# Two mixers with their order of work changed: recurrence first, attention second, in a one-core decoder trunk

## The chip, the cores and the metric

The kernel runs on one core of a Trainium2 chip. The metric is the device time of one execution in microseconds (us), median of several runs. A core has TensorE (PE in the profile: matrix products and transposes; PEld is its weight load), VectorE (DVE), ScalarE (ACT), GpSimd (POOL) and SyncE (SP, which here issues the weight transfers). Each engine works its own instructions off in the order in which they are written and waits on semaphores for the others.

## The reference

A trunk of two layers on 256 tokens of width 1024, all in fp32. The part that matters here is the mixer at the head of each layer:

```
u = rmsnorm(h, mix_norm_gain[i])
fq, fk, fv, fg, hq, hf, hi, hg = split(u @ w_in[i])
a_out = head_rmsnorm(forgetting_attention(fq, fk, fv, fg, bias), fox_gain, 8)
r_out = head_rmsnorm(hgrn2_recurrence(hq, hf, hi, lower_bounds[i]), hgrn_gain, 8) * silu(hg)
h = h + concatenate([a_out, r_out]) @ w_out[i]
```

The attention ("FoX" below) has 8 heads of 64 and a decay from the cumulated gate added to its logits. The recurrence ("HGRN") has 8 heads too: its output at t sums q_t k_s v_s over s <= t, each product decayed elementwise by the forget gates between s and t. After the mixer layer 0 has a dense SwiGLU of width 2816, layer 1 a top-2 mixture of 8 experts of width 3584; each layer ends with a gated embedding, and the trunk with a norm.

## The kernel before, in words

**Products.** Every fp32 matrix is split in a high and a low part in a reduced format, and a product is three matmuls (lines 1427 to 1429). Weights arrive as chunks of 1 MB in 7 buffers (`raw`), in the order of the list `STATIC`. Of each chunk ScalarE makes the high part (`hi_upto`, L562) and VectorE the low part (`lo_upto`, L878); SP may load chunk n only after chunk n-7 has been consumed. Tokens are 2 tiles of 128 (`t`).

**Projections of a mixer.** Of the seven 512-wide projections the gate `hg`, `fv` and `hi` are made token-major, in four quarters of 12 matmuls (a token tile and half the contraction each, `quarter`); `hf`, `fq`, `fk`, `hq` are made transposed, each in two chunks of 48 matmuls over all 256 tokens (`transposed`), between whose halves other work of TensorE can be put (`between`).

**Recurrence.** The chunkwise sum is done by levels: `step(0)` and `step(1)` make the diagonal of the score matrix of each token tile, `step(2)` to `step(8)` the blocks of 1, 2, 4 ... 64 tokens behind each other, `step(9)` the part across the two tiles. For each step TensorE does 16 or 32 small matmuls, VectorE masks the result into `scores` (`take`), and between two levels it multiplies the keys and queries by the decay over the span (`decay`, two instructions); a step waits for the decay of the level before. `recur(t)` then multiplies the scores by `hi`.

**Attention.** `pair_logits(i)` makes the logits of two of six units, VectorE finds the row maxima (`unit_max`), ScalarE the exponentials (`unit_exp`), TensorE turns them (`pair_turn`), ScalarE copies them out (`pT_out`), `attend(t)` multiplies by `fv`.

**Heads and output.** For each of four head tiles j (half, t) ScalarE squares, VectorE sums (`mean_square`), ScalarE makes the root (`head_root`), VectorE normalizes (`head_norm`, for the HGRN half with the gate besides), TensorE turns the tile (`head_turn`), VectorE multiplies by the gain (`head_gained`), ScalarE and VectorE split it (`head_hi`, `head_rest`). An `out_part(n, hf, t)` is 12 matmuls: output half n, contraction half hf, token tile t. After the last head tile the sum h of token tile 0 is formed (`add_to_h`) and normalized for the next stage (`norm(1, 0)` in layer 0, `norm_gained(0)` in layer 1, both write `un`); TensorE turns `un`, then does one more `out_part`.

**Order.** Everything is written out by hand, one list per engine: `mixer(l)` of ScalarE at L608, of VectorE at L1002, of TensorE at L1455. TensorE's list was: `hf`, `fq`, `fk`, `hq` with the logits of attention in between; then the quarters of `fv` and `hi` with the steps of the recurrence, `attend(0)` and `attend(1)` between them; head tiles in the order FoX 0, FoX 1, HGRN 0, HGRN 1; `out_part` of contraction half 0 (FoX) first.

## Time and profile before

| | before |
|---|---|
| median of 3 runs | 1603.91 us (1603.11 to 1604.16) |
| the profiled execution: span, first to last instruction | 1601.0 us |
| TensorE busy | 1523.5 us (95%) |
| VectorE, ScalarE busy | 1227.2 us (77%), 998.7 us (62%) |
| mean granted TensorE clock | 0.977 |
| mixer of layer 0, from the first product after the forget gate to the turn of the next norm | 46.05 to 174.40 us |
| the same of layer 1, start of the first logits to the end of the next `un` | 452.63 to 554.50 us |

The profile gives one execution, and its span is the only time given for it; the runs are timed from the outside, their median lies 2.9 us above that span. Times inside are from the start of the span. An end of a matmul is modelled, its start is recorded, so pieces of TensorE's work are measured from start to start. The clock is that granted to TensorE, 1.00 for full speed (2.4 GHz) and 0.50 for half of it (1.2 GHz).

### The profile page before, as it was taken

Reading aid. Unit: us, or ns where it says so; the run is one execution under the profiler, and the core shown is the slowest. Engines: PE = TensorE matmul, PEld = TensorE weight load, DVE = VectorE, ACT = ScalarE, POOL = GpSimd, SP = SyncE. Lnnn points to the kernel's source line nnn. Section 1 sums busy time; section 2 is a strip of 40 time slices with the busy share of each in tenths; the row PEclk is TensorE's granted clock in tenths of the full one; section 3 lists DMA queues with packets and bytes.
Section 4 is the critical chain, followed back from the end, with each engine's and each line's share of the span. In section 5 each row is a group of like instructions: output and inputs, shape, how many; then the busy total and the mean of one; then the engine's idle time right before and its main releaser. Section 6 shows DMA issues by size and latency. Waiting matters only on the chain.

```text
span 1601.0 us, 20998 instructions
## 1 busy us (share of the span) xinstructions
PE 1523.5 (95%) x7875; PEld 1282.4 (80%) x7875; DVE 1227.2 (77%) x1059; ACT 998.7 (62%) x842; POOL 56.7 (4%) x75
## 2 busy tenths in 40 slices
PE   6998999999998859999999999999999999999976
PEld 5986788887997758888888888888888888888855
DVE  5576654458558659889888888888988888888875
ACT  5441533446552237787787787787777787787753
POOL 4000000000000000000000000000000000000000
PEclk9999999999999869999999999999999999999997
DMA  8422465546442239999999999999999999999970
GB/s 275 158 97 65 146 218 184 184 158 209 136 145 91 101 118 375 369 376 391 370 376 392 371 374 391 368 380 386 375 374 381 373 377 388 367 376 391 373 280 27
DMA packets 206207, 451.76 MB, mean 282 GB/s; under 512 B 12424, under 2 KB 31440, under 8 KB 205904
## 3 DMA queue, kind: packets, MB, share of 16 engines
q1 hardware_dynamic: 200368, 439.48, 76.3%
q0 software_dynamic: 2592, 9.44, 1.6%
q10 hardware_dynamic: 3200, 2.20, 0.5%
q8 instruction: 32, 0.52, 0.1%
q14 instruction: 15, 0.12, 0.0%
HBM read 444.80 MB, written 6.29 MB: 282 GB/s over the span
## 4 chain that ended last, share of the span: by engine, by line
PE 77%; issue 11%; DVE 6%; ACT 2%; SPq 2%; DMA 1%; POOL 0%; POOLq 0%; DVEq 0%; ACTq 0%
PE bank L1427 24%; PE bank L1429 23%; PE bank L1428 23%; DVE wlo L878 2%; PE bank L1854 1%; PE bank L1524 1%; SPq L411 1%; PE bank L1576 1%; ACT un L548 1%; DMA raw<-in_w_exp_down_dram 1%; DVE scores L1071 0%; PE bank L1588 0%; PE bank L1836 0%; PE bank L1495 0%; PE bank L1533 0%
## 5 line engine op out<-in xcount | busy, mean ns | idle before, releaser
L878 DVE TENSOR_TENSOR wlo<-raw,whi 128x2048 fp32r<-128x2048 f32 x415 | 937.8, 2288 | 174.6 <-ACT whi L781 104.1
L781 ACT ACTIVATE whi<-raw 128x2048 fp32r<-128x2048 f32 x341 | 639.8, 1912 | 63.8 <-DMA raw<-in_w_exp_down_dram 32.0
L1427 PE MATMUL bank<-whi,uTh 128*128 128x512 f32 (+1 forms) x1312 | 523.1, 399 | 17.3 <-DVE uTl L1122 8.1
L1428 PE MATMUL bank<-wlo,uTh 128*128 128x512 f32 (+1 forms) x1312 | 512.8, 391 | 0.0
L1429 PE MATMUL bank<-whi,uTl 128*128 128x512 f32 (+1 forms) x1312 | 512.7, 391 | 0.0
L1427 PEld LDWEIGHTS bank<-whi,uTh 128*128 128x128 f32 x1312 | 249.8, 190 | 68.3 <-DVE uTl L1122 8.6
L1429 PEld LDWEIGHTS bank<-whi,uTl 128*128 128x128 f32 x1312 | 249.6, 190 | 52.9
L1428 PEld LDWEIGHTS bank<-wlo,uTh 128*128 128x128 f32 x1312 | 250.2, 191 | 48.4
L1427 PE MATMUL bank<-whi,hTr 128*128 128x512 f32 x528 | 207.3, 393 | 0.0
L1429 PE MATMUL bank<-whi,hTr 128*128 128x512 f32 x528 | 205.7, 390 | 0.0
L1428 PE MATMUL bank<-wlo,hTr 128*128 128x512 f32 x528 | 205.5, 389 | 0.0
L562 ACT ACTIVATE whi<-raw 128x2048 fp32r<-128x2048 f32 x74 | 139.1, 1914 | 1.0 <-DMA raw<-in_w_in_dram 0.9
L694 ACT ACTIVATE hTr<-bank 128x512 fp32r<-128x512 f32 x56 | 33.6, 599 | 137.1 <-PE bank L1854 137.1
L1429 PEld LDWEIGHTS bank<-whi,hTr 128*128 128x128 f32 x528 | 99.1, 188 | 20.8
L1427 PEld LDWEIGHTS bank<-whi,hTr 128*128 128x128 f32 x528 | 99.1, 188 | 20.3 <-issue 0.4
L1428 PEld LDWEIGHTS bank<-wlo,hTr 128*128 128x128 f32 x528 | 99.2, 188 | 20.1
L1427 PE MATMUL bank<-uTh,whi 128*128 128x256 f32 x256 | 73.4, 287 | 0.7 <-DVE wlo L878 0.7
L1428 PE MATMUL bank<-uTl,whi 128*128 128x256 f32 x256 | 72.4, 283 | 0.0
L1429 PE MATMUL bank<-uTh,wlo 128*128 128x256 f32 x256 | 72.4, 283 | 0.0
L736 ACT ACTIVATE hTr<-bank 128x512 fp32r<-128x512 f32 x10 | 5.4, 595 | 74.2 <-PE bank L1731 74.2
L613 ACT ACTIVATE work<-bank 128x512 f32<-128x512 f32 x24 | 14.4, 598 | 59.8 <-PE bank L1429 59.7
L1427 PEld LDWEIGHTS bank<-uTh,whi 128*128 128x128 f32 x256 | 49.1, 192 | 2.0 <-DVE wlo L878 1.1
(239 smaller groups left out, 1041.3 us busy)
## 6 DMA issues: line engine op xcount, KB each, us to landing
raw<-in_w_exp_gate_dram SPq DMA_DIRECT2D x112, 1024.0 KB, 6.3
raw<-in_w_exp_up_dram SPq DMA_DIRECT2D x112, 1024.0 KB, 6.9
raw<-in_w_exp_down_dram SPq DMA_DIRECT2D x112, 1024.0 KB, 6.4
raw<-in_w_in_dram SPq DMA_DIRECT2D x28, 1024.0 KB, 5.5
raw<-in_w_ffn_gate_dram SPq DMA_DIRECT2D x11, 1024.0 KB, 5.2
raw<-in_w_ffn_up_dram SPq DMA_DIRECT2D x11, 1024.0 KB, 5.1
raw<-in_w_ffn_down_dram SPq DMA_DIRECT2D x11, 1024.0 KB, 4.9
raw<-in_w_out_dram SPq DMA_DIRECT2D x8, 1024.0 KB, 5.2
```

The source lines that it names most:

```text
L411: sp.dma_start(as_k(raw[:, n % RAW, :], src.shape[1]), src).then_inc(filled[n % RAW], 16)
L548: nc.scalar.activation(un[:, t, :], h[:, t, :], ACT.Square, accum_out=ssq[:, t:t + 1]).then_inc(sq_done, 1)
L562: nc.scalar.activation(whi[:, n % SPLIT, :], raw[:, n % RAW, :], ACT.Copy).then_inc(hi_a, 1)
L694: nc.scalar.activation(exhT[r % 2][0], bank(4, 4, P), ACT.Copy).then_inc(exT_hi, 1)
L781: nc.scalar.activation(whi[:, s % SPLIT, :], raw[:, s % RAW, :], ACT.Copy).then_inc(hi_a, 1)
L878: return V.tensor_tensor(wlo[:, n % RAW, :], raw[:, n % RAW, :], whi[:, n % SPLIT, :].bitcast(F32), ALU.subtract).then_inc(lo_ready, 1)
L1427: T.matmul(o, sth, mvh, start=start, stop=False)
L1428: T.matmul(o, sth, mvl, start=False, stop=False)
L1429: return T.matmul(o, stl, mvh, start=False, stop=stop)
L1524: last = T.matmul(b[:, t * NP + hp, :], keyT[r, hp, t * P:(t + 1) * P], later, start=True, stop=True)
L1576: last = T.matmul(bank(FOX_BANK[t])[:, hd * HD:(hd + 1) * HD], probsT[u][:, i * nk + kt, :], fv[:, kt, hd * HD:(hd + 1) * HD], start=kt == ...
L1854: last = T.transpose(bank(4, 4, P)[:, c, :], exh[r % 2][:, c * P:(c + 1) * P], ident[:, :])
```

## The change

- The chunks of `w_in` are loaded in the order `hg`, `hf`, `hq`, `fq`, `fk`, `hi`, `fv`; those of `w_out` as (n, hf) = (1,1), (0,1), (0,0), (1,0).
- TensorE: `step(0)` to `step(7)` stand between the halves and chunks of `fq` and `fk`, 24 projection matmuls apart; `step(8)` and `step(9)` stand between quarters of `hi`. The logits of attention follow, between quarters of `hi` and `fv`, then the turns, with `recur(0)` and `recur(1)` among them; `attend(0)` and `attend(1)` stand behind the last quarter of `fv`, the first `out_part` between them.
- Head tiles run in the order HGRN 0, HGRN 1, FoX 0, FoX 1, and `out_part` starts with contraction half 1.
- `cross`, the result of `step(9)`, is copied out by ScalarE instead of VectorE, to another place. Banks of PSUM change hands (`FOX_BANK`, `HGRN_BANK`, `step_bank`).
- No product is added or removed, and the bytes loaded are the same.

```diff
-IN_ORDER = ["hg", "hf", "fq", "fk", "hq", "fv", "hi"]
+IN_ORDER = ["hg", "hf", "hq", "fq", "fk", "hi", "fv"]
+OUT_ORDER = [(1, 1), (0, 1), (0, 0), (1, 0)]
...
# ScalarE, mixer(l)
-                for j, (to, scale) in enumerate(((qT, HD ** -0.5), (kT, 1.0))):
+                hi_upto(first + 8)
+                for j, (to, scale) in enumerate(((hqT, 1.0), (qT, HD ** -0.5), (kT, 1.0))):
                     for c in range(2):
                         u = 5 + 2 * j + c
                         out_of(to[:, 2 * c:2 * c + 2, :], bank(u % 4, 2, SEQ), ACT.Copy, scale, consumed, first + u)
-                        hi_upto(first + u + 2)
+                        hi_upto(first + u + (4 if j == 0 and c == 0 else 5))
+                for par in range(2):
+                    act.wait_ge(lev[l], 2 * (STEPS - 1) + par + 1)
+                    nc.scalar.activation(cross[:, par::2, :], bank(step_bank(STEPS - 1) + par, NP, P), ACT.Copy).then_inc(cross_ready[l], 1)
+                hi_upto(first + 16)
+                out_of(hv[:, 0, :], bank(3), ACT.Copy, 1.0, tile0_in[l], 2)
                 unit_exp(l, 0)
                 unit_exp(l, 1)
...
+                head_square(l, 1, HGRN_BANK[1], hgrn_o[l], 2)
+                out_of(fv[:, 0, :], bank(1), ACT.Copy, 1.0, tile0_in[l], 3)
                 pT_out(l, 2)
                 pT_out(l, 3)
+                head_root(l, 1)
                 unit_exp(l, 4)
                 unit_exp(l, 5)
+                head_hi(l, 0)
+                out_of(fv[:, 1, :], bank(2), ACT.Copy, 1.0, consumed, first + 14)
                 pT_out(l, 4)
                 pT_out(l, 5)
...
# VectorE, mixer(l), the new list up to the heads
+                dve.wait_ge(proj_a[l], 6)
                 V.tensor_tensor(qP, hqT, fT, ALU.mult).then_inc(x_ready[l], 1)
                 dve.wait_ge(x_ready[l], 1)
                 take(0)
+                lo_upto(first + 10)
                 take(1)
                 decay(0)
                 take(2)
                 decay(1)
                 take(3)
+                lo_upto(first + 11)
                 decay(2)
                 take(4)
                 decay(3)
                 take(5)
+                lo_upto(first + 12)
                 decay(4)
                 take(6)
+                decay(5)
+                take(7)
+                lo_upto(first + 13)
+                decay(6)
+                take(8)
+                lo_upto(first + 14)
+                unit_max(0)
+                unit_max(1)
+                lo_upto(first + 15)
+                unit_max(2)
+                unit_max(3)
+                lo_upto(first + 16)
+                mean_square(0)
+                unit_max(4)
+                unit_max(5)
                 head_norm(0)
                 mean_square(1)
                 head_norm(1)
                 head_gained(0)
+                lo_upto(first + 17)
                 head_rest(0)
                 head_gained(1)
                 head_rest(1)
                 mean_square(2)
                 head_norm(2)
                 mean_square(3)
                 head_gained(2)
                 head_norm(3)
                 head_rest(2)
...
# TensorE, mixer(l): the new list (all its lines are new or moved)
+                transposed("fq", 0, lambda: step(0))
+                step(1)
+                transposed("fq", 1, lambda: step(2))
+                step(3)
+                transposed("fk", 0, lambda: step(4))
+                step(5)
+                transposed("fk", 1, lambda: step(6))
+                step(7)
+                b0 = begin()
+                quarter("hi", b0, 0, 0)
+                step(8)
+                b1 = begin()
+                quarter("hi", b1, 1, 0)
+                step(9)
+                quarter("hi", b0, 0, 1)
+                pair_logits(0)
+                quarter("hi", b1, 1, 1)
+                pair_logits(1)
+                b0 = begin()
+                quarter("fv", b0, 0, 0)
+                pair_turn(0)
+                recur(0)
+                b1 = begin()
+                quarter("fv", b1, 1, 0)
+                pair_logits(2)
+                recur(1)
+                quarter("fv", b0, 0, 1)
+                pair_turn(1)
+                head_turn(0)
+                quarter("fv", b1, 1, 1)
+                pair_turn(2)
+                head_turn(1)
+                attend(0)
+                pe.wait_ge(proj_a[l], 14)
+                out_part(1, 1, 0)
+                attend(1)
+                pe.wait_ge(uT_ready, split_before(TURN_MIX[l]) + 2)
+                out_part(0, 1, 0)
+                head_turn(2)
+                out_part(1, 1, 1)
+                out_part(0, 0, 0)
+                head_turn(3)
+                out_part(1, 0, 0)
+                out_part(0, 1, 1)
+                out_part(0, 0, 1)
                 norm(3 * l + 1, 0)
+                out_part(1, 0, 1)
```

How the lists stand in the built programs is shown for two places. The first is VectorE where the recurrence begins: L1134 (now L1123) makes `qP`, L1063 (L1062) is a `take` of step 0 or 1, L1051 and L1052 (L1050, L1051) a `decay`, L1071 (L1070) the take of a level, L878 (L877) a low part. Before:

```order
L1039 TENSOR_TENSOR bank<-bank,causal 128x2x128 [waits logits0]
L1041 TENSOR_REDUCE small<-bank 128x2 [waits dchain]
L1134 TENSOR_TENSOR work<-work 128x1024 [waits proj_a0]
L1063 COPY_PREDICATED scores<-masks,bank 128x4x128 [waits lev0,x_ready0]
L1063 COPY_PREDICATED scores<-masks,bank 128x4x128 [waits lev0]
L1063 COPY_PREDICATED scores<-masks,bank 128x4x128 [waits lev0,lev_d0]
L1063 COPY_PREDICATED scores<-masks,bank 128x4x128 [waits lev0]
L1051 TENSOR_TENSOR work<-work 128x512 [waits lev0]
L1052 TENSOR_TENSOR work<-work 128x512
L1071 COPY_PREDICATED scores<-masks,bank 128x8x64 [waits lev0,lev_d0]
L1071 COPY_PREDICATED scores<-masks,bank 128x8x64 [waits lev0]
```

With the change:

```order
L877 TENSOR_TENSOR wlo<-raw,whi 128x2048 [waits hi_a] x3
L1123 TENSOR_TENSOR work<-work 128x1024 [waits proj_a0]
L1062 COPY_PREDICATED scores<-masks,bank 128x4x128 [waits lev0,x_ready0]
L1062 COPY_PREDICATED scores<-masks,bank 128x4x128 [waits lev0]
L877 TENSOR_TENSOR wlo<-raw,whi 128x2048 [waits hi_a]
L1062 COPY_PREDICATED scores<-masks,bank 128x4x128 [waits lev0,lev_d0]
L1062 COPY_PREDICATED scores<-masks,bank 128x4x128 [waits lev0]
L1050 TENSOR_TENSOR work<-work 128x512 [waits lev0]
L1051 TENSOR_TENSOR work<-work 128x512
L1070 COPY_PREDICATED scores<-masks,bank 128x8x64 [waits lev0,lev_d0]
L1070 COPY_PREDICATED scores<-masks,bank 128x8x64 [waits lev0]
L1050 TENSOR_TENSOR work<-work 128x256x2 [waits lev0]
```

The row maxima of attention (L1039, L1041), which stood ahead of `qP`, now come after all levels, and low parts stand between the levels at other places.

The second is ScalarE at the first heads: L591 (now L593) squares a head tile, L597 and L599 (L599, L601) are its root, L613 (L615) copies a projection out, L562 makes a high part, L588 copies turned probabilities out, L583 is an exponential, L606 (L608) makes the high part of a turned head tile. Before:

```order
L591 ACTIVATE work<-bank 128x512 [waits fox_o0]
L562 ACTIVATE whi<-raw 128x2048 [waits consumed,filled2]
L597 ACTIVATE small<-small 128x8 [waits hms0]
L599 ACTIVATE small<-small 128x8 [waits hln0]
L591 ACTIVATE work<-bank 128x512 [waits fox_o0]
L613 ACTIVATE work<-bank 128x512 [waits tile0_in0]
L597 ACTIVATE small<-small 128x8 [waits hms0]
L599 ACTIVATE small<-small 128x8 [waits hln0]
L562 ACTIVATE whi<-raw 128x2048 [waits consumed,filled3]
L606 ACTIVATE uTh<-work 128x4x128 [waits tmp_ready]
L613 ACTIVATE work<-bank 128x512 [waits consumed]
L606 ACTIVATE uTh<-work 128x4x128 [waits tmp_ready]
```

With the change:

```order
L593 ACTIVATE work<-bank 128x512 [waits hgrn_o0]
L599 ACTIVATE small<-small 128x8 [waits hms0]
L601 ACTIVATE small<-small 128x8 [waits hln0]
L593 ACTIVATE work<-bank 128x512 [waits hgrn_o0]
L615 ACTIVATE work<-bank 128x512 [waits tile0_in0]
L588 ACTIVATE attT<-bank 128x512 [waits pT_psum0] x2
L599 ACTIVATE small<-small 128x8 [waits hms0]
L601 ACTIVATE small<-small 128x8 [waits hln0]
L583 ACTIVATE un,small<-bank,small 128x256 [waits pT_psum0,nmax_ready0]
L583 ACTIVATE un,small<-bank,small 128x256
L583 ACTIVATE un,small<-bank,small 128x256 [waits pT_psum0,nmax_ready0]
L583 ACTIVATE un,small<-bank,small 128x256
```

The first head tiles are now those of the recurrence (`hgrn_o`), and between their squares and their high parts stand a copy of `fv`, two copies of turned probabilities and four exponentials; the high parts of weights that stood there have gone ahead.

## Rows read from the trace of the kernel before

A row of a window view gives the stretch, its length, then for PE, PEld, DVE, ACT and POOL the busy us and (x instructions), the granted clock, the DMA share and GB/s. A row of a timeline gives start and length in us, engine, line, operation, output<-input, shapes and count, and in brackets the idle time before it with what ended it. A row of groups gives busy us and mean ns of one, then the idle time before.

**Rows 1.** PE busy and granted clock in the tail of the mixer, layers 0 and 1 (windows).
```profile
120.00:180.00 60.00, 51.44 (x335) 43.14 (x334) 41.48 (x69) 19.65 (x26) 0.00 (x0) 0.91 0.28 90
500.00:560.00 60.00, 51.21 (x339) 43.35 (x338) 38.72 (x67) 17.04 (x25) 0.00 (x0) 0.91 0.30 100
```

**Rows 2.** PE timeline, layer 0: the two waits of the tail.
```profile
139.08 0.80 PE L1427 MATMUL bank<-whi,uTh 128*128 128x512 f32 x1 [4.03 <-DVE uTl L1122]
...
144.36 1.16 PE L1533 MATMUL bank<-work 64*128 64x128 f32 x16
...
161.53 1.12 PE L1597 MATMUL bank<-ident,un 128*128 128x128 f32 x4 [4.53 <-DVE un L1103]
162.30 0.78 PE L1427 MATMUL bank<-whi,uTh 128*128 128x512 f32 x1
```

**Rows 3.** Windows: granted clock in the 2 us behind the first of them.
```profile
138.00:140.00 2.00, 0.92 (x2) 0.82 (x3) 1.63 (x3) 0.34 (x1) 0.00 (x0) 0.50 0.00 0
```

**Rows 4.** PE timeline, layer 0: starts from which pieces are priced.
```profile
46.05 0.47 PE L1427 MATMUL bank<-uTh,whi 128*128 128x256 f32 x1
...
72.24 0.49 PE L1554 MATMUL bank<-work 64*128 64x128 f32 x4
...
88.80 0.47 PE L1427 MATMUL bank<-whi,uTh 128*128 128x512 f32 x1
...
91.74 0.38 PE L1533 MATMUL bank<-work 64*128 64x128 f32 x2
...
102.41 2.00 PE L1524 MATMUL bank<-work 64*128 64x64 f32 x32
104.35 0.50 PE L1427 MATMUL bank<-whi,uTh 128*128 128x512 f32 x1
...
112.10 1.89 PE L1576 MATMUL bank<-work,attT 128*128 128x64 f32 x16
```

**Rows 5.** Timeline, layer 0: towards the next norm, ScalarE, VectorE, TensorE.
```profile
165.35 3.73 ACT L562 ACTIVATE whi<-raw 128x2048 fp32r<-128x2048 f32 x2
...
172.38 0.81 DVE L906 TENSOR_SCALAR un<-h,small 128x1024 f32<-128x1024 f32 x1
...
174.40 1.03 PE L1422 MATMUL bank<-ident,un 128*128 128x128 f32 x8
```

**Rows 6.** VectorE groups of layer 0's mixer, 46.05 to 174.4 us.
```profile
L878 DVE TENSOR_TENSOR wlo<-raw,whi 128x2048 fp32r<-128x2048 f32 x14 | 32.1, 2290 | 7.2 <-ACT whi L562 7.1
L1071 DVE COPY_PREDICATED scores<-masks,bank 128x512 f32<-128x512 uint32 x14 | 11.5, 884 | 0.0
L1051 DVE TENSOR_TENSOR work<-work 128x512 f32<-128x512 f32 x7 | 4.8, 685 | 5.6 <-PE bank L1524 5.6
```

**Rows 7.** ScalarE groups of the same stretch.
```profile
L562 ACT ACTIVATE whi<-raw 128x2048 fp32r<-128x2048 f32 x14 | 26.7, 1912 | 0.0
L613 ACT ACTIVATE work<-bank 128x512 f32<-128x512 f32 x10 | 6.0, 600 | 28.7 <-PE bank L1429 28.7
```

**Rows 8.** DMA issues: the chunks of `w_in` (count, KB each, us to landing).
```profile
raw<-in_w_in_dram SPq DMA_DIRECT2D x28, 1024.0 KB, 5.5
```

**Rows 9.** Timeline, layer 1: the same places, TensorE, ScalarE, VectorE.
```profile
452.63 0.49 PE L1554 MATMUL bank<-work 64*128 64x128 f32 x4
...
541.41 0.90 PE L1597 MATMUL bank<-ident,un 128*128 128x128 f32 x3 [4.74 <-DVE un L1103]
...
545.23 3.72 ACT L781 ACTIVATE whi<-raw 128x2048 fp32r<-128x2048 f32 x2
550.87 1.06 ACT L548 ACTIVATE un<-h 128x1024 f32<-128x1024 f32 x1 [1.93 <-DVE h L986]
...
553.22 1.28 DVE L913 SCALAR_TENSOR_TENSOR un<-h,small,work 128x1024 f32<-128x1024 f32 x1
```

**Rows 10.** Windows: 2 us around a short wait ahead of layer 1's mixer.
```profile
406.00:408.00 2.00, 0.25 (x1) 0.25 (x2) 1.59 (x3) 1.98 (x3) 0.00 (x0) 1.00 0.00 0
```
**Rows 11.** PE timeline, layer 1: the instruction behind that short wait.
```profile
407.75 0.50 PE L1427 MATMUL bank<-whi,uTh 128*128 128x512 f32 x1 [2.33 <-DVE uTl L939]
```

171 lines of the change are left out of this document (52 added, 119 removed).

## The prediction

> **What bounds the kernel now.** I read the busy table first: TensorE is busy 95% of the span, and dense products carry most of it. A change of order adds and removes no product, so it can only take away time in which TensorE waits, or in which it works at the lower clock because it had waited. I then looked for such time where the change is. In the last 60 us of each mixer TensorE is busy about 51 us and the mean clock is 0.91 [rows 1]: the reader is to see that 9 us of waiting and a slow stretch lie there, in both layers alike, while neither VectorE nor ScalarE is full. The timeline gives the places in layer 0. After the turn of the second FoX head TensorE waits 4.03 us for the low part of a turned head tile, and after the second recurrence 4.53 us for `un`, the last head of the HGRN half [rows 2]. Both are chains over three engines with too little product work beside them. Behind the first wait the clock is granted at 0.50 [rows 3]. The 12 products that begin at 139.08 take 5.28 us to the next piece [rows 2] where the same 12, from 88.80 to 91.74, take 2.94 [rows 4]: 2.3 us lost. After the second, the head turn takes 0.77 us [rows 2], and I put 1.4 us on the slow start of it and of the products behind it: from 162.30 to the turn at 174.40 [rows 5] 48 matmuls take 12.10 us, against about 11.05 for four groups at the full pace of 0.23 us a matmul. So of the 128.35 us from 46.05 [rows 4] to 174.40 [rows 5], 8.6 are waits and 3.7 low clock, and 116.0 are work that the change can't touch.
>
> **The levels among the query and key products.** Prices of TensorE: 216 matmuls of a transposed projection take 26.2 us from 46.05 to 72.24, so half a chunk (24) takes 2.9; a level takes 1.94 (102.41 to 104.35) [rows 4]. With 0.1 us for each change of kind, levels come every 5.0 us. VectorE has per level two multiplications of 0.68 and two masked copies of 0.88, 3.1 us, and a low part of 2.29 in every second or third [rows 6], on average under 4.3. It keeps up. The tightest place is `step(5)`: from the end of `step(3)` VectorE must do a decay, a take (of narrow blocks, so I allow 2.5 against a mean of 1.8), the low part of chunk 11 and another decay, 1.4 + 2.5 + 2.3 + 1.4 = 7.5 us; TensorE has half a chunk, a level and half a chunk, 7.8 to 8.0. Covered, by about 0.5 us. I count no wait here; if it fails, it costs the difference once, so 0 to 1 us a layer. TensorE's products need weights ahead: ScalarE makes high parts in 1.91 us and copies results out in 0.60 [rows 7], and its list before `cross` asks for 2.5 us in each 5 to 10 us of TensorE. SP may load chunk n once chunk n-7 is consumed: the last of the mixer, chunk 17, goes out when `hi`'s first chunk is done at 103.6 and lands in about 5.5 us [rows 8], 5 us before ScalarE asks for it; the chunks before it have more. Layer 1's VectorE starts its levels some 2 us later in the same pattern, since it has the lower bounds to apply, and meets `step(2)` in time. The cross copies are two of 0.6 us on ScalarE [rows 7]; TensorE passes `step(9)` at about 104.7 and needs them at 112.6, so they are hidden by a quarter of `hi`, logits and another quarter; without that cover they would cost 1.2. VectorE loses two copies of the same length there and gains nothing by it, as it waits at this point anyway.
>
> **The new tail, walked for layer 0.** From 46.05 I lay the pieces out in the new order at the same prices (12 products with their change of kind 2.94; `attend(0)`, 16 recorded matmuls, 1.85, and `attend(1)`, 32 of them, 3.6 [rows 4], the two `recur` alike; a head turn 0.42 and a pair of turned units 0.85, a little more than their matmuls at the same pace). The second tile-0 quarter of `fv` ends at 131.4. Behind it ScalarE has a copy (0.6), two copies of probabilities (1.1 to 1.8 with the turn that they wait for) and a root (0.45), to 133.7; VectorE then normalizes and gates HGRN tile 1 (2.2), to 135.9, multiplies tile 0 by the gain (0.68), makes the low part of chunk 17 (2.29) and only then the low part of tile 0 (0.68), to 139.5. TensorE meanwhile does a pair of turns, a head turn, a quarter, a pair of turns, a head turn and `attend(0)`, to 138.8. **First new wait: 0.7.** `attend(1)` ends at 146.1. TensorE then has `out_part(0,1,0)`, the turn of FoX tile 0 and `out_part(1,1,1)`, to 152.3. From the end of that turn (149.6) the chain is gain 0.68, high part 0.63, root 0.42, norm of the last tile 1.5, low part 0.68, to 153.5. **Second: 1.2.** The turn of the last head tile thus starts at 46.05 + 107.3 (the 116.0 less that turn and three output parts, 8.7) + 1.9 of waits + about 1.0 for ten more changes between product kinds = 156.3, where it was 161.53 [rows 2].
>
> **The finish line.** Everything after the mixer hangs on `un` of the next norm. Before, it ended 173.19 (172.38 + 0.81), 11.66 us after the last head turn had begun: a gain, a high part, a table load, two high parts of weights to 169.08, a low part, the sum, the norm [rows 5]. That chain doesn't shrink, but for 0.35 us of slow head turn: 156.3 + 11.3 = 167.6. TensorE now arrives with only three output parts behind the head turn instead of four, at 165.0. **Third new wait: 2.6**, where it had arrived 1.2 late before (174.40). What follows (gain, split, products of the next stage) keeps its distance from `un`. Layer 0 gains 173.2 - 167.6 = **5.6 us**. Behind it stand dense products with TensorE as the bound, so the gain stays.
>
> **Layer 1** runs 380.4 us later (452.63 against 72.24 [rows 4, 9]) and identically up to the tail: the last head turn starts at 156.3 + 380.4 = 536.7 instead of 541.41. There `un` ended at 554.50. From the head turn to the end of the two high parts, 548.95, it was 7.54 [rows 9], less 0.35; that gives 543.9, earlier than which the norm can't start. The sum is formed by then (the first output half is done at about 540). From the start of the norm at 550.87 to the end of `un` it was 3.63 [rows 9]: 547.5. Before, TensorE's slow clock had held the sum back by 1.9 us more. Gain: 554.5 - 547.5 = **7.0 us**. After it comes the routing, a chain of VectorE, ScalarE and DMA from `un`, with no other anchor: it moves as a whole, and the experts after it are bound by products.
>
> **Sum.** 5.6 + 7.0 = 12.6 us off the span of 1601.0: 1588.4. The median of the runs lies 2.9 above that span, so 1591.3. Bounds: without any of the new waits another 3.8 + 3.1 would go (up to 1584.5), which needs chains shorter than any row shows; with both chains of the tail 1.5 us longer in each layer it is 1597.3.
>
> **A price not shown: the clock after short waits.** I charge none. The nearest rows: a wait of 2.33 us ahead of layer 1's mixer leaves the clock at 1.00 [rows 10], and the matmul behind it is recorded with 0.50 us [rows 11], while the one behind 4.03 us has 0.80 at a clock of 0.50 [rows 2, 3]. The new waits are 0.7, 1.2 and 2.6, so nearest to the first; 2.6 lies between. If they did drop the clock, each would cost up to the 2.3 us above. The Trainium skill says otherwise for one pattern (TensorE: Matmul & The Clock Gate, "A second HAM failure mode: psum-queue depth-cycling"): frequent small idles between groups of matmuls can make the clock swing between its two levels. By that rule the sum would be 9.2 us smaller, four drops of 2.3; at the one short wait shown here the trace doesn't agree.
>
> **Rivals.** (A) The forecast, waits as walked: 60%, on its own 1587 to 1595. (B) The tail's chains are longer, since ScalarE's list puts copies and exponentials ahead of the HGRN root, and an engine that stands at a wait holds all behind it: two waits a layer longer by 1 to 2 us, gain 5 to 8, 1596 to 1599: 18%. For it: two chains have under 1 us of room. Against: VectorE idles over 10 us between 105 and 134 in my walk. (C) Less waiting than walked, about 1586: 5%. (D) The clock drops at the second and third wait of each layer, 4 x 2.3 given back: 1600.5, half of it on either side of the bound of "same": 10%. (E) No change: new waits as long as the old ones in the same two places, clock drops included: 1604: 3%. (F) Slower: the two old waits come back at their old size before the first and fourth output parts, each with its slow stretch, and the wait before the norm (2.6), which is new, comes on top in both layers: 1603.9 + 5.2 = 1609. It decides from the point at which the chain into the first output part is 3.3 us and that into the FoX half 2.8 us longer than walked, for instance if a high part is late and VectorE stands at the low part of chunk 17 with the turned head behind it. Against it: that chunk's high part is due some 20 us earlier. 4%.
>
> **Numbers.** 1591.3 is the forecast of the likeliest case. The range, 1586 to 1600, takes in A, B and C and half of D, and leaves out E and F. A measurement of this kernel tells 0.2% from no change, 3.2 us, so faster means under 1600.7: A + B + C + half of D = 0.88; same 0.08; slower 0.04.
>
> **What would show it.** Right: the waits of 4.03 and 4.53 are gone; the last head turn of layer 0 starts near 156, `un` ends near 167.6 (layer 1: 547.5); the clock stays at 1.00 from 60 to 175; a wait of 2 to 3 us stands before the norm's turn. Wrong: a level (L1513 now) that waits for a decay by over 1 us; a clock of 0.50 after a wait under 3 us (D); a wait over 3 us at the first or fourth output part (B, F); or a gain in the mixers that is given back in the routing or the experts.

## The result, and the profile after

The changed kernel takes 1590.53 us, the median of 4 runs (1590.46 to 1592.08), against 1603.51 us of the kernel before in 4 runs beside it. The ratio is 0.9917, with a 95% interval of 0.9905 to 0.9929, so it is faster by 13 us, or 0.8%. The forecast was 1591.3, in a range of 1586 to 1600. The profiled execution has a span of 1590.3 us (the run of 1592.08); the three others have 1588.7 to 1588.8. In all four the time lies 1.8 us above the span.

**The tail of layer 0.** The two waits of 4.03 and 4.53 us [rows 2] are gone. Three shorter ones stand in their place. The timeline of TensorE in the changed kernel (products are lines 1422 to 1424 now, the turn of a head tile L1591, the turn of the next norm L1417):

```profile
140.85 0.47 PE L1422 MATMUL bank<-whi,uTh 128*128 128x512 f32 x1 [0.65 <-issue]
...
154.60 0.50 PE L1422 MATMUL bank<-whi,uTh 128*128 128x512 f32 x1 [1.23 <-DVE uTl L1119]
...
157.46 0.38 PE L1591 MATMUL bank<-ident,un 128*128 128x128 f32 x2
...
168.66 1.57 PE L1417 MATMUL bank<-ident,un 128*128 128x128 f32 x8 [2.39 <-DVE un L905]
```

The profile calls the releaser of the first wait "issue", that is, nothing that it can name. VectorE's list shows what it is: the low part of chunk 17 stands ahead of the low part of the turned head tile, which ends at 140.74, 0.11 us before TensorE goes on.

```profile
137.86 2.28 DVE L877 TENSOR_TENSOR wlo<-raw,whi 128x2048 fp32r<-128x2048 f32 x1
140.06 0.68 DVE L1119 TENSOR_TENSOR uTl<-work,uTh 128x512 fp32r<-128x512 f32 x1
```

The matmul behind each of the first two takes 0.47 and 0.50 us, where behind the old wait it took 0.80 [rows 2]. Behind the third the turn takes 1.57 us instead of the 1.03 of before [rows 5]. The window views say the same: the granted clock over the tail rose from 0.91 [rows 1], and fell in one place only.

```profile
46.00:120.00 74.00, 74.00 (x687) 67.63 (x685) 57.22 (x69) 32.32 (x43) 0.00 (x0) 1.00 0.39 129
120.00:190.00 70.00, 65.41 (x358) 55.01 (x357) 42.09 (x73) 30.73 (x57) 0.00 (x0) 0.98 0.30 95
168.00:174.00 6.00, 5.34 (x21) 4.54 (x22) 5.90 (x8) 3.48 (x4) 0.00 (x0) 0.72 0.47 171
404.00:408.00 4.00, 4.00 (x12) 3.17 (x11) 2.36 (x2) 3.89 (x3) 0.00 (x0) 0.58 0.02 4
```

From 46 to 120 us, where the levels stand among the products, TensorE is busy 74.00 of 74 us at full clock. So it was in the kernel before, where the levels stood among other products:

```profile
46.00:120.00 74.00, 74.00 (x639) 67.88 (x637) 49.08 (x62) 35.71 (x63) 0.00 (x0) 1.00 0.37 123
```

Up to 120 us the new places of the levels thus gain nothing; what is gained in layer 0 is gained behind it, where the last four steps of the recurrence stood before (at 122.3, 127.2, 132.5 and 144.4 us) and none stands now. The row of 404 us is new and has nothing to do with the tail. It lies behind a wait of 2.33 us ahead of layer 1's mixer, which the kernel before had too, and at a clock of 1.00 [rows 10, 11].

```profile
403.16 0.50 PE L1422 MATMUL bank<-whi,uTh 128*128 128x512 f32 x1 [2.33 <-DVE uTl L938]
```

**The finish lines.** The timelines of VectorE and ScalarE in layer 0, towards the next norm; they answer to [rows 5]:

```profile
159.47 1.28 ACT L705 ACT_TABLE_LOAD   x1
160.76 3.73 ACT L564 ACTIVATE whi<-raw 128x2048 fp32r<-128x2048 f32 x2
165.64 1.06 ACT L550 ACTIVATE un<-h 128x1024 f32<-128x1024 f32 x1 [1.15 <-DVE h L985]
```
```profile
162.71 2.29 DVE L877 TENSOR_TENSOR wlo<-raw,whi 128x2048 fp32r<-128x2048 f32 x1 [1.93 <-ACT whi L564]
164.92 0.68 DVE L985 TENSOR_TENSOR h<-bank,h 128x512 f32<-128x512 f32 x1
...
167.79 0.81 DVE L905 TENSOR_SCALAR un<-h,small 128x1024 f32<-128x1024 f32 x1
```

In layer 1, TensorE's turns of the two norms and its first product of the experts:

```profile
544.10 1.09 PE L1417 MATMUL bank<-ident,un 128*128 128x128 f32 x8 [1.78 <-DVE un L912]
...
554.56 1.97 PE L1417 MATMUL bank<-ident,un 128*128 128x128 f32 x8 [4.49 <-DVE un L912]
...
578.12 0.79 PE L1422 MATMUL bank<-whi,uTh 128*128 128x512 f32 x1 [1.60 <-DVE uTl L1349]
```

**Where the 10.7 us between the two spans lie.** Layer 0's mixer began 1.43 us later (47.48 against 46.05). That comes from a second slow stretch, behind a wait for a low part of weights at 31 us. The products go on at 31.11 us here and at 31.16 in the kernel before; from there to the mixer it is 16.37 us against 14.89. The matmul behind the wait, and the windows over 6 us of the changed kernel, of the kernel before and of the changed kernel run again (e0 below):

```profile
31.11 0.39 PE L1422 MATMUL bank<-uTh,whi 128*128 128x256 f32 x1 [1.77 <-DVE wlo L877]
```
```profile
31.00:37.00 6.00, 5.88 (x36) 5.89 (x37) 4.53 (x3) 2.20 (x2) 0.00 (x0) 0.72 0.70 226
31.00:37.00 6.00, 5.84 (x48) 5.84 (x49) 4.60 (x3) 3.34 (x3) 0.00 (x0) 1.00 0.81 266
31.00:37.00 6.00, 5.11 (x42) 5.11 (x43) 5.33 (x3) 3.47 (x3) 0.00 (x0) 1.00 0.82 273
```

`un` of layer 0 ended at 168.60 instead of 173.19: 4.59 earlier, so 6.02 gained from the mixer's start. The slow stretch at 404 us cost 1.63 (24 products and the change behind them in 7.20 us against 5.57, start to start). `un` of layer 1 ended at about 544.05 instead of 554.50, 10.45 earlier, which is 4.59 - 1.63 + 7.49. The experts began 10.44 earlier (588.56 before) and the span is 10.7 shorter: the routing and the experts gave nothing back.

### The profile page after: what moved, and what is told of

The parts are those of the page before. It is cut to its first block, busy times and chain, and to the rows that moved or that the text cites. A ratio compares the mean times of both kernels' runs of the same rounds, so it can differ in the third digit from the quotient of the medians.

```text
span 1590.3 us, 20999 instructions
## 1 busy us (share of the span) xinstructions
PE 1521.0 (96%) x7875; PEld 1281.2 (81%) x7875; DVE 1223.7 (77%) x1055; ACT 995.9 (63%) x846; POOL 56.4 (4%) x75
## 4 chain that ended last, share of the span: by engine, by line
PE 80%; issue 10%; DVE 4%; ACT 2%; SPq 2%; DMA 1%; POOL 0%; POOLq 0%; DVEq 0%; ACTq 0%
PE bank L1422 24%; PE bank L1424 24%; PE bank L1423 24%; PE bank L1513 2%; DVE wlo L877 2%; PE bank L1854 1%; SPq L413 1%; PE bank L1568 1%; ACT un L550 1%; PE bank L1836 0%; PE bank L1582 0%; PE bank L1490 0%; PE bank L1522 0%; PE bank L1417 0%; PE bank L1546 0%
## 5 line engine op out<-in xcount | busy, mean ns | idle before, releaser
L877 DVE TENSOR_TENSOR wlo<-raw,whi 128x2048 fp32r<-128x2048 f32 x415 | 936.3, 2288 | 164.6 <-ACT whi L780 100.8
L615 ACT ACTIVATE work<-bank 128x512 f32<-128x512 f32 x24 | 14.3, 596 | 64.1 <-PE bank L1424 64.0
```

The costliest lines, as they stand in the source:

```text
L877: return V.tensor_tensor(wlo[:, n % RAW, :], raw[:, n % RAW, :], whi[:, n % SPLIT, :].bitcast(F32), ALU.subtract).then_inc(lo_ready, 1)
```

## The experiments

All are edits of the changed kernel. They ran in three groups, each with the kernel before beside it: its median was 1603.88 us beside e0 to e3, 1604.67 beside e4 to e8, and 1605.28 beside e10 and e11. Medians of different groups are therefore better compared by their ratios, whose intervals reach 2 to 3 us to either side; effects smaller than that are read from pieces of the timelines. No run puts the heads of attention first again or the levels back to their old places, so what each of these two parts gives alone is not shown. Since the cost ahead of the mixers varies from one execution to the next, I read pieces from start to start of TensorE's timeline, from the turn of the first head tile (L1591) in each layer: to the turns of the next stage's two norms, and on to the wait ahead of layer 1's mixer, or to the experts' first product. Norm 0 and norm 1 are those of token tiles 0 and 1. A few line numbers differ between the kernels.

| us from the first head turn | L0: norm 0 | L0: norm 1 | L0: mixer of L1 | L1: norm 0 | L1: norm 1 | L1: experts | ratio to before |
|---|---|---|---|---|---|---|---|
| changed kernel | 34.88 | 46.07 | 269.38 | 34.31 | 44.77 | 68.33 | 0.9917 |
| the same again (e0) | 34.91 | 46.11 | 269.41 | 34.35 | 44.81 | 68.26 | 0.9913 |
| e2, low part later | 34.07 | 45.26 | 268.56 | 33.47 | 43.92 | 67.54 | 0.9906 |
| e4, norm later | 36.67 | 47.87 | 271.17 | 36.07 | 46.53 | 69.79 | 0.9932 |
| e5, norm first, layer 0 | 32.36 | 44.70 | 269.58 | 34.35 | 44.81 | 68.41 | 0.9916 |
| e6, norm first, layer 1 | 34.89 | 46.08 | 269.38 | 32.37 | 40.62 | 64.89 | 0.9890 |
| e8, low part before norm | 33.35 | 44.55 | 267.85 | 32.79 | 43.25 | 66.98 | 0.9893 |
| e10, combined | 29.99 | 39.07 | 262.33 | 30.00 | 38.25 | 60.55 | 0.9812 |

These distances repeat within 0.1 us between the first two rows, much better than whole runs do.

### e0: the changed kernel again

No edit.

> The changed kernel once more, to learn what of its profile is the kernel and what the one execution. If the clock of 0.50 behind the wait of 2.33 us ahead of layer 1's mixer belongs to the kernel, it shows again and the span is about 1590.3; if it belongs to that one execution, the clock there stays at 1.00, the span is about 1588.7 (1.6 us less), and the median is 1590.5 again. The same for the later start of layer 0's mixer (1.4 us): as noise it changes, as part of the change it is 1.4 again.

Median 1590.36 us (1589.25 to 1591.08), ratio 0.9913 (0.9899 to 0.9926), span 1589.3. The windows behind the wait, which is 2.34 us here:

```profile
402.50:404.50 2.00, 2.00 (x6) 1.57 (x7) 0.00 (x0) 1.99 (x2) 0.00 (x0) 0.59 0.03 8
404.50:406.50 2.00, 2.00 (x7) 1.57 (x6) 1.57 (x1) 2.00 (x2) 0.00 (x0) 0.55 0.00 0
```

The drop came again, and yet the span is 1.0 shorter. What is missing is the other slow stretch: the wait at 31 us is 1.25 us here, the clock behind it stays at 1.00, and the mixer begins 14.87 us behind it, at 46.76 instead of 47.48. So the drop at 404 us showed again, and the late start was noise. Over the twelve profiles of this study (the section on the hardware) neither drop is in every execution of the changed kernel or of its edits, and neither is a single accident. The kernel before has neither in its one profile, which can't tell how often it would.

### e1: the cross block copied by VectorE

```diff
-                for par in range(2):
-                    act.wait_ge(lev[l], 2 * (STEPS - 1) + par + 1)
-                    nc.scalar.activation(cross[:, par::2, :], bank(step_bank(STEPS - 1) + par, NP, P), ACT.Copy).then_inc(cross_ready[l], 1)
...
                 take(8)
+                for par in range(2):
+                    dve.wait_ge(lev[l], 2 * (STEPS - 1) + par + 1)
+                    V.tensor_copy(cross[:, par::2, :], bank(step_bank(STEPS - 1) + par, NP, P)).then_inc(cross_ready[l], 1)
```

> The two copies of the cross block go back from ScalarE to VectorE. My reading: TensorE needs them 3.5 us after step(9) at the earliest and both engines have room, so the time stays within 0.5 us of the changed kernel and the three waits of the tail are the same. Rival: VectorE's list from the levels to the first head (unit_max, mean_square) is what feeds the chain into the first output part; then two copies of 0.6 more on it make that wait 0.65 + 1.2 and the kernel 1 to 2.4 us slower.

Median 1590.91 us (1589.40 to 1592.54), ratio 0.9915 (0.9899 to 0.993). The waits of the tail are 0.65, 1.22 and 2.39. This part of the change is worth nothing that can be measured; both engines had the room.

### e2: the low part of chunk 17 behind the turned heads

```diff
                 head_gained(0)
-                lo_upto(first + 17)
                 head_rest(0)
                 head_gained(1)
                 head_rest(1)
+                lo_upto(first + 17)
```

> The low part of chunk 17 is moved behind the second turned head on VectorE. By the prediction it is the 2.29 us of it that make the chain into the first output part too long by 0.65 us: the wait there is gone in both layers, 1.3 us in all, and if nothing else becomes late the kernel is faster by 1.0 to 1.3. The second wait (1.2) stays as it is. Rival: the wait recorded there is no wait for this chain but the change between kinds of matmul; then it stays at 0.65 and the time is the same. A second rival: what TensorE saves there it waits for at the second wait, whose chain starts from VectorE and ScalarE and not from TensorE; then the second wait grows to about 1.9 and the time is the same.

Median 1588.91 us (1587.13 to 1590.35), ratio 0.9906 (0.9892 to 0.9919). The first wait is gone in both layers and the second is still 1.23. It was thus the low part of the head tile, late behind 2.29 us of weights. Both layers' norms come 0.84 and 0.88 us earlier: 0.2 more than the idle time recorded.

### e3: the levels in series

```diff
-                transposed("fq", 0, lambda: step(0))
-                step(1)
-                transposed("fq", 1, lambda: step(2))
-                step(3)
-                transposed("fk", 0, lambda: step(4))
-                step(5)
-                transposed("fk", 1, lambda: step(6))
-                step(7)
+                transposed("fq", 0)
+                transposed("fq", 1)
+                transposed("fk", 0)
+                transposed("fk", 1)
+                for s in range(8):
+                    step(s)
```

> Steps 0 to 7 of the recurrence stand one behind the other after the query and key products instead of between them; all else is as in the changed kernel. If the products between the levels hide VectorE's work, it is now open: in each of steps 3 to 7 TensorE stands for the two decay multiplications (1.4 us and the signals, about 1.6), and twice for a low part of 2.3 us in VectorE's list, some 12 us a layer, 20 to 28 us in all, with a lower clock on top. If the levels in their new place were worth little (the gain of the change comes from the tail alone), it is under 5 us.

Median 1628.78 us (2 runs), ratio 1.0154 (1.0135 to 1.0172): slower than the kernel before, and 38 us slower than the changed one. Two of TensorE's levels, and two windows (the products ahead of them, then the levels):

```profile
88.01 3.27 PE L1513 MATMUL bank<-work 64*128 64x64 f32 x32 [2.49 <-DVE work L1051]
92.70 3.68 PE L1513 MATMUL bank<-work 64*128 64x64 f32 x32 [1.42 <-DVE work L1051]
```
```profile
46.00:80.00 34.00, 34.00 (x285) 33.97 (x284) 15.21 (x22) 19.38 (x17) 0.00 (x0) 1.00 0.52 171
88.00:112.00 24.00, 17.74 (x160) 17.00 (x160) 17.66 (x20) 0.00 (x0) 0.00 (x0) 0.51 0.00 1
```

A level waits 1.4 us for the decay, and 2.0 to 2.5 where a low part stands in VectorE's list: 9.45 us of waits in layer 0. I had expected some 12. What I had only put "on top" is as large: between such waits the clock stays at 0.50, and a level takes 3.67 us where the same 32 matmuls take 2.00 in the changed kernel. Five levels lose 8 us by that, the products behind them 1.7. The products between the levels hide both: from the start of the mixer's projections to the first head turn it is 18.1 us more in layer 0 and 19.1 in layer 1. This is the price of having no products between the levels. It is no part of the 13 us of the change, since the kernel before had products between them too.

### e4: the norm later

```diff
             act.wait_ge(h_ready[1], 2)
-            norm(1, 0)
             hi_upto(out0 + 6)
+            norm(1, 0)
...
-            for n in range(2):
+            for n in range(3):
                 hi(n, 0)
```

(and `hi(2, 0)` leaves its place behind the norm of layer 1's tile 0)

> One high part of weights more (1.91 us of ScalarE) stands ahead of the first norm behind each mixer. If the finish line is un of that norm, as predicted, un of layer 0 and of layer 1 come 1.9 us later, the waits before its turn become 4.3 and 3.7 us and the kernel is slower than the changed one by 3.8 us, and by up to 1.7 more a layer if the clock now falls behind them: 1594 to 1598. If TensorE's own work is the finish line and the wait is only beside it, the time stays at 1590.5.

Median 1593.18 us (1592.76 to 1596.47), ratio 0.9932 (0.9917 to 0.9947). The waits are 4.19 and 3.58 us, and both norms of both layers come 1.7 to 1.8 us later (the table). By the ratios the kernel is 3.0 us slower than the changed one (3.3 by the distances) where 3.8 were expected, and the median lies just below the expected 1594 to 1598: the size was somewhat too large, the mechanism is the one expected. So the chain ScalarE, VectorE, `un` is a finish line, as predicted, and not TensorE's work beside it. The clock fell to 0.50 behind both waits and the distance from the first norm to the second did not change (11.20 and 10.46, as in e0): there it cost nothing.

### e5: the norm first in layer 0

```diff
             nc.scalar.preload_act_table(ACT.Sqrt)
-            hi_upto(out0 + 5)
             act.wait_ge(h_ready[1], 2)
             norm(1, 0)
-            hi_upto(out0 + 6)
+            hi_upto(out0 + 5)
...
             add_to_h(0, 0, bank(0), h_ready[1])
-            lo_upto(out0 + 4)
             dve.wait_ge(first_out[0], 2)
             add_to_h(0, 1, bank(2), h_ready[1])
             norm(1, 0)
-            lo_upto(out0 + 5)
+            lo_upto(out0 + 4)
             gains(TURN_NORM[1], 0, norm_rows(1))
+            lo_upto(out0 + 5)
```

> Behind layer 0's mixer the norm goes ahead of everything that doesn't feed it: the two high parts on ScalarE and the low part on VectorE come after it. The sum can then be complete at about 161.6 and un at 164.5 on the clock of the changed kernel's profile, before TensorE ends its output parts at 166.27: the wait of 2.39 goes, and the kernel is faster than the changed one by 2.2 to 2.4 us (1588.2). Rival: the delayed low parts are then late for the first gate product; a wait of 1 to 2 us appears within 6 us behind the norm's turn and half of the gain or all is given back.

Median 1591.32 us (1590.63 to 1592.93), ratio 0.9916 (0.9902 to 0.9929): no gain. The wait of 2.39 is gone, and another stands before the turn of the second norm:

```profile
178.73 1.27 PE L1416 MATMUL bank<-ident,un 128*128 128x128 f32 x8 [2.87 <-DVE un L904]
```
```profile
169.99 2.28 DVE L876 TENSOR_TENSOR wlo<-raw,whi 128x2048 fp32r<-128x2048 f32 x1
172.19 0.68 DVE L984 TENSOR_TENSOR h<-bank,h 128x512 f32<-128x512 f32 x1
172.80 2.28 DVE L876 TENSOR_TENSOR wlo<-raw,whi 128x2048 fp32r<-128x2048 f32 x1
175.00 0.68 DVE L984 TENSOR_TENSOR h<-bank,h 128x512 f32<-128x512 f32 x1
```

Half right, then: the rival of a delayed low part was the right kind of thing, but in the wrong place. The first norm came 2.55 us earlier; the second only 1.4, since the displaced low parts now stood ahead of the second tile's sum; and behind the new wait the clock was 0.57 from 179 to 183 us, where a product matmul is recorded with 0.63 us instead of 0.39, and that lost the rest. Tile 1 has a finish line of its own, which the first wait had covered.

### e6: the norm first in layer 1

```diff
-            for n in range(2):
-                hi(n, 0)
             for t in range(TT):
                 act.wait_ge(h_ready[4], 2 * t + 2)
                 norm(MOE_NORM, t)
+                if t == 0:
+                    hi(0, 0)
...
             add_to_h(1, 0, bank(1), h_ready[4])
-            lo(1, 0)
             dve.wait_ge(consumed, done(("out", 1, 1, 0)))
...
             ungained_turn(1)
-            for n in range(2, LEAD):
-                lo(n, 0)
+            lo(1, 0)
...
             link(V.tensor_tensor(g2, gexp, g1, ALU.mult))
+            for n in range(2, LEAD):
+                lo(n, 0)
```

(and `hi(1, 0)` behind `un` of tile 0)

> The same behind layer 1's mixer: norm of tile 0 ahead of the two high parts on ScalarE, the sum and norm of tile 1 ahead of the low part of the experts' second chunk, and the third and fourth low part after the routing, while TensorE waits for the gathered tokens. First wait 1.78 gone (TensorE is busy to 542.3), second wait 4.5 down to about 2.4, so the routing and the experts start 3.5 to 4 us earlier: 1586.8. Rival: a low part stands ahead of a step of the routing, or is late at the experts' first products; then the gain is under 2 us and the expert's first chunks show waits.

Median 1587.75 us (1585.18 to 1589.64), ratio 0.9890 (0.9875 to 0.9905). The first wait is gone, the second is 2.32, and the second norm comes 4.19 us earlier. Of this 0.8 was lost at the experts, the rival in small: the two low parts (4.49 us) stood ahead of the tokens' low part, and the wait before the first product became 3.52 instead of 1.60.

### e8: the turned tile's low part before the last norm

```diff
                 head_gained(2)
-                head_norm(3)
                 head_rest(2)
+                head_norm(3)
```

> VectorE makes the low part of the turned FoX tile 0 before it normalizes the last head tile, instead of behind it. The low part is then ready at about 152.7 where TensorE comes at 153.4, so the second wait (1.23) goes in both layers; the last tile's norm comes about 0.4 to 0.7 us later, with 3 us of products ahead of its turn. Faster than the changed kernel by 2.2 to 2.5 us (1588.1). Rival: the last norm becomes late and the wait moves to the last head turn, and the time is the same within 0.5.

Median 1588.75 us (1585.60 to 1589.45), ratio 0.9893 (0.9878 to 0.9908). The second wait is gone in both layers, the last head turn is not late, and each norm comes 1.56 us earlier, 0.33 more than the idle time recorded. By the ratios that is 3.2 us less than the changed kernel, where 2.2 to 2.5 were expected.

### e11: the output products behind all heads

```diff
                 attend(0)
                 pe.wait_ge(proj_a[l], 14)
-                out_part(1, 1, 0)
                 attend(1)
-                pe.wait_ge(uT_ready, split_before(TURN_MIX[l]) + 2)
-                out_part(0, 1, 0)
                 head_turn(2)
-                out_part(1, 1, 1)
-                out_part(0, 0, 0)
                 head_turn(3)
+                out_part(1, 1, 0)
+                pe.wait_ge(uT_ready, split_before(TURN_MIX[l]) + 2)
+                out_part(0, 1, 0)
+                out_part(1, 1, 1)
+                out_part(0, 0, 0)
```

> The third part of the change undone: TensorE does the output products of the HGRN half only behind the turns of both FoX heads instead of around attend(1) and the turn of FoX tile 0. The chain from a FoX head's end to its turn (square, mean, root, norm, about 5.6 us) is then covered by attend(1) alone: a wait of about 2 us at the first FoX turn and 2 more at the last, against the waits of 0.65 and 1.23 that go: 2 to 3 us a layer, 4 to 6 in all, 1594.5 to 1596.5. If the output products were no needed cover, it is the same within 1 us.

Median 1595.90 us (1594.78 to 1596.31), ratio 0.9940 (0.9925 to 0.9955). TensorE waits before both FoX turns, in both layers alike, the second time longer than the 2 us expected:

```profile
144.78 0.66 PE L1591 MATMUL bank<-ident,un 128*128 128x128 f32 x4 [1.90 <-DVE un L1097]
148.97 1.12 PE L1591 MATMUL bank<-ident,un 128*128 128x128 f32 x4 [3.54 <-DVE un L1097]
```

Having the HGRN half ready to multiply while the FoX heads are normalized is thus worth 1.7 us in layer 0 and 2.7 in layer 1 by the distances of the table (271.15 and 70.98), which is 4.4 in all; the ratios give 4.3.

### e10: what the others point to, together

e2 and e8, and the weights' parts taken out of the stretch behind the mixer, into time in which their engines stand; in layer 1 the low parts as in e6, with one instead of two before the tokens:

On ScalarE:

```diff
                 head_root(l, 3)
+                early()
                 head_hi(l, 3)
...
+            mixer(0, lambda: hi_upto(STATIC.index(("out", 0, *OUT_ORDER[0])) + 5))
...
-            hi_upto(out0 + 5)
             act.wait_ge(h_ready[1], 2)
             norm(1, 0)
```

On VectorE (in layer 1 the early parts are those of the experts' first two chunks, and of the first one):

```diff
                 head_norm(3)
+                early()
                 head_gained(3)
...
+            mixer(0, lambda: lo_upto(STATIC.index(("out", 0, *OUT_ORDER[0])) + 4))
...
             add_to_h(1, 0, bank(1), h_ready[1])
-            lo_upto(out0 + 6)
             dve.wait_ge(consumed, done(("out", 0, 1, 0)))
             add_to_h(1, 1, bank(3), h_ready[1])
+            lo_upto(out0 + 6)
             norm(1, 1)
```

> All that the runs so far point to, on top of the changed kernel: the low part of chunk 17 behind the turned heads (no wait of 0.65), the low part of FoX tile 0 ahead of the last head's norm (no wait of 1.23), and, since norm first in layer 0 only moved the wait to tile 1, the weights' parts not behind the norm but ahead of it, in time in which their engines stand: two high parts on ScalarE and one low part on VectorE ahead of the last turned head, where ScalarE idles 6.5 us and VectorE 3.6; the low part that stood between the two sums of tile 1 goes behind them; in layer 1 one low part only stands while TensorE waits for tokens. Layer 0: waits of 0.65, 1.23, 2.39 and 0.3 gone, 4.2 to 4.6 us. Layer 1: 0.65, 1.23, 1.78 gone and the second norm 2.3 earlier, 5.5 to 6 us. Together about 10 us less than the changed kernel: 1580.5, range 1579 to 1584. If the norm of tile 1 stays late in layer 0 (a wait over 1 us), 1582 to 1584.

Median 1574.71 us (1573.93 to 1579.20), ratio 0.9812 (0.9796 to 0.9829), span 1573.4: below the expected range, and the fastest version, 15.7 us below the changed kernel (e0; 16.2 by the ratios) and 30.6 below the one before (1605.28 beside it). ScalarE makes the two high parts before the last head tile is even turned, and the norm starts at 158.09:

```profile
150.27 3.71 ACT L564 ACTIVATE whi<-raw 128x2048 fp32r<-128x2048 f32 x2
155.32 0.63 ACT L608 ACTIVATE uTh<-work 128x512 fp32r<-128x512 f32 x1 [1.34 <-DVE work L1116]
...
158.09 1.06 ACT L550 ACTIVATE un<-h 128x1024 f32<-128x1024 f32 x1 [0.84 <-DVE h L988]
```

TensorE has no wait at all in layer 0's tail. I had added up 4.2 to 4.6 us for layer 0 and 5.5 to 6 for layer 1; the table has 7.1 and 7.7. In layer 0 the missing part is the second norm: it follows the first by 9.08 us instead of 11.20, because no low part stands between the two sums of tile 1 any more, and TensorE's own work between the norms is only those 9.08. In layer 1 it is 1.15 us from the second norm to the experts (22.30 against 23.45), where the router's second tile stands behind one low part instead of two. The rest is the 0.2 to 0.3 us by which each wait costs more than is recorded. Its profile has no slow stretch ahead of layer 1's mixer, which is worth another 1.6 and is chance.

## Why the prediction was right

**The levels cost no wait.** They come every 5.00 us (70.47, 75.47, 80.47, 85.47) at full clock. At the tightest, `step(5)`, VectorE's decay ends at 84.54 and the level starts at 85.47: 0.9 us of room where I had counted 0.5. The last row of VectorE's decay and the start of the level, in layer 0:

```profile
83.85 0.69 DVE L1051 TENSOR_TENSOR work<-work 128x512 f32<-128x512 f32 x1
```
```profile
85.47 0.33 PE L1513 MATMUL bank<-work 64*128 64x64 f32 x2
```

The prediction rightly called this covered but put no price on what the products hide; e3 does, 18 to 19 us a layer, half of it clock.

Nothing is gained in this stretch itself: the kernel before has no wait from 46 to 120 us either.

**The walk of the tail held.** The waits forecast as 0.7, 1.2 and 2.6 were 0.65, 1.23 and 2.39. The chains were named rightly too: e2 removed the first by moving the low part of chunk 17, e8 the second by moving the low part of tile 0 ahead of the last head's norm. The last head turn was forecast for 156.3 and came at 157.46, of which 1.43 is the later start.

**The finish line.** `un` of layer 0 was forecast at 167.6 and ended at 168.60, or 167.2 without the later start; the gain was 6.0 instead of 5.6. In layer 1 it was 7.5 instead of 7.0. The end forecast for it, 547.5, was on the clock of the kernel before and left out the 5.6 us that layer 0 gains; with them it is 541.9, and 544.05 was measured, later by the two slow stretches (1.4 and 1.6) and earlier by the 0.9 gained beyond the forecast. e4 shows that this chain is what TensorE waits for. What the step left out is that the second tile has such a chain too. It made no difference here, since the second norm kept its distance of 11.2 us; e5 shows where it does.

**The clock after short waits** was charged with nothing. For 0.65 and 1.23 us this was right, here and in every other profile. For the wait of 2.4 it was wrong in this execution: clock 0.50 behind it. The prediction had named this as a sign of being wrong, and it was seen. It cost nothing here, as e0 shows, where the clock stayed at 1.00 in the same place and the second norm came after the same 11.20 us. What TensorE does faster there it then waits for:

```profile
172.75 0.50 PE L1422 MATMUL bank<-whi,uTh 128*128 128x512 f32 x1 [0.95 <-DVE uTl L938]
...
179.16 1.09 PE L1417 MATMUL bank<-ident,un 128*128 128x128 f32 x8 [0.67 <-DVE un L905]
```

The two drops that did cost, 1.5 us at 33 and 1.6 at 405, lie ahead of the two mixers, where the prediction didn't look for any. For the second I had taken [rows 10] as proof that a wait of 2.33 leaves the clock alone. That window ends 0.25 us behind the wait and shows little; the clock did stay at 1.00 in that execution (from 408 to 412 us too), but it was one outcome of two. So the mechanism of case D exists, but in the tail for the third wait alone and not always, and there it is paid for by time that the second norm waits for anyway. That the charge of nothing held is in part luck.

The rule of the Trainium skill weighed there (TensorE: Matmul & The Clock Gate, "A second HAM failure mode: psum-queue depth-cycling") does not describe the tail of this kernel. e3 comes nearer to it, with idles of 1.4 to 2.5 us between groups, but there the clock didn't swing: it was 0.51 over 24 us.

**The sum.** 12.6 us were forecast from the span. The profiled pair shows 10.7: 6.0 + 7.5, less 1.4 of start and 1.6 of clock, +0.2. The medians show 13.0. The two differ because the profiled execution of the changed kernel, with both slow stretches, is 1.6 us above its median, and that of the kernel before (1601.0, with the same 1.8 us from span to time) 0.7 below. So the 2.9 us that the forecast put on top of the span were 1.8 of offset and 1.1 of chance. The bound for the case without new waits does not come out of the walk: it put 3.8 us on layer 0, where the waits add up to 4.5 (0.7 + 1.2 + 2.6). e10, which removes them and more, gained 7.1 and 7.7 us, far beyond that bound of 1584.5.

**The rivals.** B and F needed long waits in the tail; there were 0.65 and 1.23, at the first and the fourth. The new wait before the norm, F's last element, was there, but the other two were small.

## What to carry to other kernels

Where every engine works off a list, look in each chain that TensorE waits for at what stands ahead of the chain's next instruction without feeding it. Here these were the high and low parts of weights, 1.9 and 2.3 us each, which had 6.5 and 3.6 us of idle time some microseconds earlier; moving them, and one low part of a head, gave 14.8 us by the distances of the table, more than the change under study. A chain of several engines between small matmuls is cheapest between dense products, and its price in series is its waits and about as much again in clock. And after a wait is removed, find the next finish line before counting the gain: in layer 0 the first norm gave nothing until the second was moved too.

## What the runs showed of the hardware

**The clock behind one wait between dense products.** Over the twelve profiles, from the mixer of layer 0 to the routing, the places where TensorE waits once in an otherwise busy stretch: behind waits of 0.65, 1.22 to 1.26 and 1.35 us the clock was 1.00 every time, and in the seven profiles with a wait of 1.78 or 1.79 in layer 1 as well. Behind 2.33 or 2.34 us ahead of layer 1's mixer it fell to 0.50 in five profiles (both of the changed kernel, e1, e3, e5) and stayed at 1.00 in seven (before, e2, e4, e6, e8, e10, e11). Behind 2.39 or 2.40 us in layer 0 it fell in five (the changed kernel, e1, e2, e6, e8) and stayed in two (e0, e3). Behind 2.87 us and more it always fell. The wait at 31 us, ahead of layer 0's mixer, is of another length in each profile: behind 0.50 to 1.48 us the clock stayed in eight, and behind 1.77 (the changed kernel), 1.97 (e1), 2.01 (e5) and 2.39 us (e8) it fell. So the length alone doesn't decide: 1.77 us was enough at 31 us, and 1.78 never was in layer 1. (The wait for the second norm of layer 1 stands behind small matmuls and is left out, and so are the pairs of e11.) At 2.33 and at 2.39 us the instructions around the wait are the same each time, so what decides lies outside the kernel's order; what it is I did not find out. Where the products behind it are the bound it costs 1.5 to 1.6 us, which is as much as the runs of one kernel differ. The place ahead of layer 1's mixer in e2, where it stayed:

```profile
400.90:402.90 2.00, 1.96 (x9) 1.62 (x10) 0.00 (x0) 1.99 (x2) 0.00 (x0) 1.00 0.04 8
402.90:404.90 2.00, 2.00 (x10) 1.68 (x9) 1.49 (x1) 2.00 (x2) 0.00 (x0) 1.00 0.00 0
```

**A wait costs more than its idle time.** Removing recorded idles of 0.65 and 1.22 us brought 0.84 and 1.56 us. Without a wait, a group of matmuls starts 0.07 to 0.24 us before the modelled end of the one ahead; a wait takes this overlap away as well. That accounts for most of the difference; the rest is not shown.
